# An announced jump for TensorE's expert loop, and the third chunk of gate and up over four column tiles

## The chip, the cores and the metric

The kernel runs on one core of a Trainium2 chip. The metric is the device time of one execution in microseconds. TensorE's full clock is 2.4 GHz; the profile shows the granted clock as a share of it.

## The reference

One inference step of two layers over 256 new and 32 continued frames (288 rows of width 1024), all in float32. Each layer is an attention mix and then a feed-forward part. Layer 0 has a dense SwiGLU, layer 1 a mixture of eight SwiGLU experts, two for each row. The change touches the experts alone:

```python
def moe(h, router, wg, wu, wd):
    logits = jnp.einsum('btd,de->bte', h, router).astype(jnp.float32)
    vals, idx = lax.top_k(logits, TOP_K)
    gates = jax.nn.softmax(vals, axis=-1)
    comb = ...
    for e in range(N_EXPERTS):
        out = out + comb[..., e:e + 1] * swiglu(h, wg[e], wu[e], wd[e])

def swiglu(h, wg, wu, wd):   # wg, wu: 1024 x 2816, wd: 2816 x 1024
    return jnp.einsum('btf,fd->btd', jax.nn.silu(h @ wg) * (h @ wu), wd)
```

## The kernel before, in words

**The experts.** Up to 96 rows (SLOTS) that chose an expert are gathered and worked on together. TensorE's array is cut into four column tiles of 32 (GRAN). Three of them (MAIN) each hold 32 of the 96 rows and multiply the main columns of a weight slice; the fourth does the slice's last columns, the tail, for the three groups in turn. Its results lie in partitions 96 to 127 of PSUM, those of the three main tiles in 0 to 95. The function `lanes` (line 2290) issues this for one slice of 128 weight rows: per PSUM bank of 512 columns first the main tiles (line 2297), then the tails that start in that bank (line 2302). The profile shows each float32 matmul as two passes, each with a weight load (LDWEIGHTS) of 32 columns of the rows; the weights of the expert are what streams.

**Chunks and units.** The 2816 columns of gate and up are cut into chunks of 1024, 1024 and 768 (WIDTH). TAIL is a quarter of the chunk, rounded down to whole 128s: 256, 256 and 128; LANE_W, the main part, is 768, 768 and 640. `project` takes one unit of a chunk, two slices; a chunk has four units of gate and four of up, so 16 slices. `down` multiplies by the down weights in slices of 1024 columns, cut 768 + 256, in four units per chunk (KUNIT: 2, 2, 2, 2 slices, and 2, 2, 1, 1 for the third chunk).

**Between gate/up and down.** ScalarE takes Silu of gate (line 1231), VectorE multiplies by up (line 1752) and gives `act_m`. `turn_chunk` (line 2317) transposes it on TensorE in blocks of 128 columns (line 2321), one transpose for 128 rows where the block has tail rows and one for 96 rows where it has none: 6, 6 and 5 transposes. `turned_parts` (line 557) gives the copies that ScalarE (line 1237) and VectorE (line 1758) then make into `am`: the main rows as they are, the tail rows regrouped into slots behind them.

**Order of the work.** TensorE's order in an expert is written out by hand in `expert(j, final)`: gate and up of chunk 0; half of gate of chunk 1; `turn_chunk(0)`; the rest of gate and up of chunk 1; down of chunk 0; half of gate of chunk 2; `turn_chunk(1)`; the rest of gate and up of chunk 2; `turn_rows` (the next expert's rows, line 2260); down(1,0) and down(1,1); `turn_chunk(2)`; down(1,2) and down(1,3); down of chunk 2.

**The loops.** TensorE, ScalarE, VectorE and GpSimd each have a loop of their own over the experts and the last expert outside it: with one round, seven iterations and one more body, hence six jumps back and one loop exit. The loop of TensorE opens in line 2405:

```python
            last = pe.snap(more * NE + (NE - 1))
            with pe.Fori(0, last) as j:
                expert(j, False)
            expert(last, True)
```

**The weights.** SyncE loads them in units of two slices (1 MB, in the third chunk 768 KB) into a ring of 12 places (line 722). It issues a unit when TensorE has used the one 12 places back (`unit_used`), and TensorE waits for a unit in `wait_unit`. An expert has 36 units.

Of the kernel before, what the change touches and what calls it, by code (L numbers as in the profile page):

```python
# [22 lines left out]
ALU = mybir.AluOpType  # L23
ACT = mybir.ActivationFunctionType
# [35 lines left out]
CHUNKS = (DFF + CW - 1) // CW  # L60
WIDTH = [min(CW, DFF - CW * c) for c in range(CHUNKS)]
KUNIT = [[2, 2, 2, 2], [2, 2, 2, 2], [2, 2, 1, 1]]
TAIL = [w // (MAIN + 1) // P * P for w in WIDTH]
LANE_W = [w - t for w, t in zip(WIDTH, TAIL)]
D_TAIL = D // (MAIN + 1)
D_LANE = D - D_TAIL
SPARE = TOK + P
# [151 lines left out]
def build(nc, a, out, consts):  # L219
# [35 lines left out]
    with ExitStack() as ctx:  # L255
# [123 lines left out]
        slot_row = carve("slot_row", 1, dt=U32)  # L379
        row_at = carve("row_at", 4)  # L380
        xr = carve("xr", D)
        sgm = carve("sgm", max(LANE_W))
        act_m = carve("act_m", max(LANE_W))
        am = carve("am", 2, CW // P, SLOTS)
        y_out = carve("y_out", D)
        sel = carve("sel", 3, P, dt=F32R)
# [166 lines left out]
        def wide(b, rows=P):  # L553

            return ps[0:rows, b:b + 2, :].rearrange("p a b -> p (a b)")

        def turned_parts(c, bank):

            n, m = TAIL[c] // P, LANE_W[c] // P
            s0, s1 = 4 * bank, min(4 * bank + 4, m)  # L560
            src = ps[:, 4 + bank, :].rearrange("p (s c) -> p s c", c=P)
            parts = [(am[:, c % 2, s0:s1, :], src[:, 0:s1 - s0, 0:SLOTS])]
            for i in range(n):
                gs = [g for g in range(MAIN) if s0 <= n * g + i < s1]
                if gs:
                    at_ = n * gs[0] + i - s0
                    dst = am[:, c % 2, m + i, GRAN * gs[0]:GRAN * (gs[-1] + 1)].rearrange("p (g c) -> p g c", c=GRAN)
                    parts.append((dst, src[:, at_:at_ + n * (len(gs) - 1) + 1:n, SLOTS:P]))
            return parts
# [337 lines left out]
        def _(act):  # L907
# [314 lines left out]
            def expert(j, final):  # L1222

                A(warm[:, 0:1], warm[:, 0:1], ACT.Silu)

                def silu(c):

                    act.wait_ge(unit_used, j * len(EXPERT) + (unit["gate", c, 3] + 1))
                    if c:
                        act.wait_ge(act_done, j * CHUNKS + c)  # L1230
                    A(sgm[:, 0:LANE_W[c]], wide(0)[:, 0:LANE_W[c]], ACT.Silu).then_inc(silu_done, 1)

                def turned(c):

                    act.wait_ge(aT_full, j * CHUNKS + (c + 1))
                    for dst, src in turned_parts(c, 0):
                        ins = A(dst, src, ACT.Copy)  # L1237
                    ins.then_inc(aT_first, 1)

                def output():  # L1240

                    act.wait_ge(row_moved, j + 1)
                    act.wait_ge(unit_used, j * len(EXPERT) + len(EXPERT))
                    for g in range(MAIN):
                        ins = A(y_out[GRAN * g:GRAN * g + GRAN, D_LANE:D], wide(6)[SLOTS:P, D_TAIL * g:D_TAIL * g + D_TAIL], ACT.Copy)
                    ins.then_inc(y_tail, 1)
                    A(y_out[0:SLOTS, 0:D_LANE], wide(6)[0:SLOTS, 0:D_LANE], ACT.Copy, scale=slot_gate[0:SLOTS, 0:1])
                    act.wait_ge(y_tail, j + 1)
                    A(y_out[0:SLOTS, D_LANE:D], y_out[0:SLOTS, D_LANE:D], ACT.Copy, scale=slot_gate[0:SLOTS, 0:1]).then_inc(y_taken, 1)

                def last_output():

                    act.wait_ge(row_moved, j + 1)
                    act.wait_ge(y_half, 1)
                    A(y_hi[0:SLOTS, 0:512], ps[0:SLOTS, 6, :], ACT.Copy, scale=slot_gate[0:SLOTS, 0:1]).then_inc(y_high, 1)
                    for g in range(MAIN):
                        if D_TAIL * (g + 1) > 512:
                            act.wait_ge(y_half, 2)
                        ins = A(y_out[GRAN * g:GRAN * g + GRAN, D_LANE:D], wide(6)[SLOTS:P, D_TAIL * g:D_TAIL * g + D_TAIL], ACT.Copy)
                    ins.then_inc(y_tail, 1)  # L1260
                    A(y_hi[0:SLOTS, 512:D_LANE], ps[0:SLOTS, 7, 0:D_LANE - 512], ACT.Copy, scale=slot_gate[0:SLOTS, 0:1]).then_inc(y_high, 1)
                    act.wait_ge(y_tail, j + 1)
                    A(y_hi[0:SLOTS, D_LANE:D], y_out[0:SLOTS, D_LANE:D], ACT.Copy, scale=slot_gate[0:SLOTS, 0:1]).then_inc(y_high, 1)

                silu(0)
                turned(0)
                silu(1)
                turned(1)
                silu(2)
                if not final:  # L1270
                    act.wait_ge(xgT_full, j + 2)
                    tokens_first_half(j + 2, 4)
                turned(2)
                if final:
                    last_output()
                else:
                    output()
# [8 lines left out]
        def _(dve):  # L1286
# [460 lines left out]
            def expert(j, final):  # L1747

                def activations(c):
                    dve.wait_ge(silu_done, j * CHUNKS + (c + 1))  # L1750
                    dve.wait_ge(unit_used, j * len(EXPERT) + (unit["up", c, 3] + 1))
                    V.tensor_tensor(act_m[:, 0:LANE_W[c]], sgm[:, 0:LANE_W[c]], wide(2)[:, 0:LANE_W[c]], ALU.mult).then_inc(act_done, 1)  # L1752

                def turned(c):

                    dve.wait_ge(aT_full, j * CHUNKS + (c + 1))
                    for dst, src in turned_parts(c, 1):
                        ins = V.tensor_copy(dst, src)
                    ins.then_inc(aT_second, 1)

                if not final:
                    picks(bass.ds(j + 1, 1))
                activations(0)
                if not final:
                    dve.wait_ge(row_moved, j + 1)
                    table(j + 2)
                turned(0)
                activations(1)
                turned(1)
                activations(2)  # L1770
                if not final:
                    dve.wait_ge(xgT_full, j + 2)
                    tokens_second_half(5)
                turned(2)
# [29 lines left out]
        def _(pe):  # L1804
# [481 lines left out]
            def expert(j, final):  # L2286
# [2 lines left out]

                    pe.wait_ge(unit_in[u % MOE_RING], j * MOE_FILLS + 16 * (u // MOE_RING + 1))  # L2290

                def lanes(b, x, w, main, tail, first, last):

                    for c0 in range(0, main, 512):
                        c1 = min(c0 + 512, main)
                        for g in range(MAIN):
                            ins = mm_(ps[GRAN * g:GRAN * g + GRAN, b + c0 // 512, 0:c1 - c0], x[:, GRAN * g:GRAN * g + GRAN], w[:, c0:c1],  # L2297
                                      start=first, stop=last)
                        for g in range(MAIN):
                            at_ = tail * g  # L2300
                            if c0 <= at_ < c1:
                                ins = mm_(ps[SLOTS:P, b + c0 // 512, at_ - c0:at_ - c0 + tail], x[:, GRAN * g:GRAN * g + GRAN],  # L2302
                                          w[:, main:main + tail], start=(first and at_ == c0),
                                          stop=(last and (g == MAIN - 1 or at_ + tail >= c1)))
                    return ins

                def project(kind, c, h):

                    u, wd = unit[kind, c, h], WIDTH[c]
                    wait_unit(u)  # L2310
                    w = unit_at(u)[:, 0:2 * wd].rearrange("p (k c) -> p k c", k=2)
                    for k in (2 * h, 2 * h + 1):
                        ins = lanes(0 if kind == "gate" else 2, xg[:, k, :], w[:, k % 2, :], LANE_W[c], TAIL[c], k == 0, k == KD - 1)
                    ins.then_inc(unit_used, 1)

                def turn_chunk(c):

                    pe.wait_ge(act_done, j * CHUNKS + (c + 1))
                    for k in range(LANE_W[c] // P):
                        r = P if k < MAIN * TAIL[c] // P else SLOTS  # L2320
                        ins = tr(ps[:, 4 + k // 4, (k % 4) * P:(k % 4) * P + r], act_m[0:r, k * P:(k + 1) * P], ident[0:r, 0:r])  # L2321
                    ins.then_inc(aT_full, 1)

                def wait_turned(c):
# [4 lines left out]
                def down(c, h):  # L2329
# [3 lines left out]
                    wait_unit(u)  # L2333
                    w = unit_at(u)[:, 0:n * D].rearrange("p (k c) -> p k c", k=n)
                    for k in range(n):
                        ins = lanes(6, am[:, c % 2, k0 + k, :], w[:, k, :], D_LANE, D_TAIL, c == 0 and h == 0 and k == 0, u == len(EXPERT) - 1 and k == n - 1)
                    ins.then_inc(unit_used, 1)

                for half in range(2):
# [62 lines left out]
                    ins.then_inc(y_half, 1)  # L2402

            last = pe.snap(more * NE + (NE - 1))
            with pe.Fori(0, last) as j:
                expert(j, False)
            expert(last, True)

# [78 lines left out]
```

## Time and profile before

| | |
|---|---|
| median of 3 runs | 1301.41 us (1300.61 to 1302.55) |
| the profiled execution | 1301.46 us |
| its span, first to last instruction | 1299.6 us |
| mean granted clock | 0.984 |
| TensorE busy | 1252.6 us, 96% of the span |
| VectorE, ScalarE, GpSimd busy | 24%, 23%, 6% |
| chain that ended last | TensorE 91%, "issue" 3%, VectorE 3%, DMA 2%, ScalarE 2% |
| stretch of the eight experts | from 516.89 us to about 1291 us |

"Issue" is time in which an engine waited for nothing that the profile shows. The chain is followed back from the last instruction. In rows of instructions, PE is TensorE's matmuls, PEld its weight loads, DVE is VectorE, ACT is ScalarE, POOL is GpSimd and SP is SyncE; a q behind the name is that engine's instruction queue. 128*32 is the part of the array in use (rows by columns) and 128x512 the operand that streams through it.

### The profile page before, as it was taken

How to read it: one execution, taken by the hardware profiler on the slowest of the kernel's cores; microseconds unless marked ns; L12 is line 12 of the kernel's file. 1: busy time of each engine (PE TensorE's matmuls, PEld its weight loads, DVE VectorE, ACT ScalarE, POOL GpSimd, SP SyncE). 2: the span in 40 equal slices, each digit the busy share in tenths (PEclk: the TensorE clock that was granted, in tenths of full speed). 3: DMA queues.
4: the chain of work that ended last, by engine and by line, in shares of the span. 5: the costliest groups of instructions: out<-in, count | busy, mean ns of one | idle time of the engine just before them, and what ended most of it. 6: DMA issues, size and time to landing. Idle time of an engine off the chain costs nothing.

```text
span 1299.6 us, 30531 instructions
## 1 busy us (share of the span) xinstructions
PE 1252.6 (96%) x13609; PEld 890.9 (69%) x13609; DVE 314.2 (24%) x632; ACT 301.7 (23%) x594; POOL 78.9 (6%) x175
## 2 busy tenths in 40 slices
PE   8999999999999999998998998998998999899998
PEld 5466799999964756675675675675675675576775
DVE  1677444443335675000000000000000000000001
ACT  2467433332334654001001001001001001000101
POOL 4231000000001020000000000000000000000100
PEclk9999999999999999999999999999999999899999
DMA  8251475544230626999999999999999999999991
GB/s 284 62 145 34 153 236 162 162 146 147 72 119 1 131 100 262 399 405 401 362 346 384 346 354 383 339 358 379 341 353 379 358 344 375 352 350 370 393 404 70
DMA packets 124228, 349.76 MB, mean 269 GB/s; under 512 B 8400, under 2 KB 33840, under 8 KB 124096
## 3 DMA queue, kind: packets, MB, share of 16 engines
q1 hardware_dynamic: 118896, 335.55, 71.8%
q0 software_dynamic: 3648, 10.60, 2.9%
q8 instruction: 118, 1.93, 0.6%
q10 hardware_dynamic: 1552, 1.56, 0.4%
q14 instruction: 14, 0.11, 0.0%
HBM read 339.65 MB, written 8.04 MB: 268 GB/s over the span
## 4 chain that ended last, share of the span: by engine, by line
PE 91%; issue 3%; DVE 3%; DMA 2%; ACT 2%; SPq 0%; DVEq 0%; ACTq 0%
PE ps L2297 34%; PE ps L2302 21%; PE ps L2209 11%; PE ps L1953 8%; PE ps L2225 5%; DMA ring<-in_w_in 2%; PE ps L2321 1%; PE ps L2026 1%; PE ps L2034 1%; PE ps L2086 1%; PE ps L2101 1%; PE ps L2139 1%; PE ps L2149 1%; PE ps L1966 1%; PE ps L2050 1%
## 5 line engine op out<-in xcount | busy, mean ns | idle before, releaser
L2297 PE MATMUL ps<-ring,xg 128*32 128x512 f32 (+2 forms) x2688 | 293.3, 487 | 30.3 <-issue 30.3
L2302 PE MATMUL ps<-ring,xg 128*32 128x256 f32 (+1 forms) x1344 | 277.2, 362 | 0.0
L2297 PE MATMUL ps<-ring_more,xg 128*32 128x512 f32 (+2 forms) x1920 | 200.6, 465 | 0.0
L2297 PEld LDWEIGHTS ps<-ring,xg 128*32 128x32 f32 x2688 | 115.6, 113 | 96.5 <-issue 62.7
L2302 PE MATMUL ps<-ring_more,xg 128*32 128x256 f32 (+1 forms) x960 | 181.7, 338 | 0.0
L2302 PEld LDWEIGHTS ps<-ring,xg 128*32 128x32 f32 x1344 | 145.7, 113 | 34.7 <-issue 5.7
L1752 DVE TENSOR_TENSOR act_m<-sgm,ps 128x768 f32<-128x768 f32 (+1 forms) x24 | 21.8, 909 | 515.4 <-PE ps L2302 415.2
L2302 PE MATMUL ps<-ring_more,am 128*32 128x256 f32 x636 | 140.1, 379 | 0.0
L2297 PE MATMUL ps<-ring_more,am 128*32 128x512 f32 (+1 forms) x1272 | 139.8, 486 | 0.0
L1953 PE MATMUL ps<-ring,hT 128*128 128x512 f32 x256 | 115.2, 596 | 0.3 <-issue 0.2
L2302 PEld LDWEIGHTS ps<-ring_more,xg 128*32 128x32 f32 x960 | 99.5, 110 | 20.3
L2297 PEld LDWEIGHTS ps<-ring_more,xg 128*32 128x32 f32 x1920 | 77.5, 110 | 43.2 <-issue 21.2
L1237 ACT ACTIVATE am<-ps 128x384 f32<-128x384 f32 (+1 forms) x64 | 16.6, 327 | 380.6 <-PE ps L2321 380.6
L2209 PE MATMUL ps<-hT_hi,w_hi 128*128 128x288 f32 x352 | 104.3, 296 | 0.5 <-DVE hT_lo L1645 0.5
L2209 PE MATMUL ps<-hT_lo,w_hi 128*128 128x288 f32 x352 | 103.8, 295 | 0.0
L2209 PE MATMUL ps<-hT_hi,w_lo 128*128 128x288 f32 x352 | 103.5, 294 | 0.0
L1303 DVE TENSOR_TENSOR w_lo<-ring,w_hi 128x2048 fp32r<-128x2048 f32 (+1 forms) x34 | 75.8, 2230 | 96.1 <-ACT w_hi L918 96.1
L2302 PE MATMUL ps<-ring,am 128*32 128x256 f32 x384 | 85.7, 380 | 0.0
L2297 PE MATMUL ps<-ring,am 128*32 128x512 f32 (+1 forms) x768 | 85.6, 486 | 0.0
L2302 PEld LDWEIGHTS ps<-ring_more,am 128*32 128x32 f32 x636 | 69.3, 110 | 22.4
L918 ACT ACTIVATE w_hi<-ring 128x2048 fp32r<-128x2048 f32 (+1 forms) x34 | 63.3, 1863 | 82.2 <-PE ps L2209 44.1
L1953 PEld LDWEIGHTS ps<-ring,hT 128*128 128x128 f32 x256 | 46.9, 190 | 51.9 <-issue 51.7
(358 smaller groups left out, 1558.0 us busy)
## 6 DMA issues: line engine op xcount, KB each, us to landing
ring<-in_moe_w_up SPq DMA_DIRECT2D x48, 1024.0 KB, 7.3
ring_more<-in_moe_w_down SPq DMA_DIRECT2D x48, 1024.0 KB, 8.2
ring<-in_moe_w_gate SPq DMA_DIRECT2D x32, 1024.0 KB, 8.0
ring_more<-in_moe_w_gate SPq DMA_DIRECT2D x32, 1024.0 KB, 8.7
ring<-in_moe_w_down SPq DMA_DIRECT2D x32, 1024.0 KB, 6.9
ring_more<-in_moe_w_gate SPq DMA_DIRECT2D x32, 768.0 KB, 7.4
ring<-in_moe_w_up SPq DMA_DIRECT2D x32, 768.0 KB, 4.9
ring_more<-in_moe_w_up SPq DMA_DIRECT2D x16, 1024.0 KB, 7.6
```

What stands on the lines that cost most here:

```text
L918: A(hi[:, 0:size], src[:, 0:size], ACT.Copy).then_inc(hi_ready, 1)
L1237: ins = A(dst, src, ACT.Copy)
L1303: V.tensor_tensor(lo[:, 0:size], src[:, 0:size], hi[:, 0:size].bitcast(F32), ALU.subtract).then_inc(lo_ready, 1)
L1752: V.tensor_tensor(act_m[:, 0:LANE_W[c]], sgm[:, 0:LANE_W[c]], wide(2)[:, 0:LANE_W[c]], ALU.mult).then_inc(act_done, 1)
L1953: ins = mm_(pair(key), hT[:, k, TOFF[t]:TOFF[t] + P], slot(wk, 4, 512)[:, k % 4, :], start=(k == 0), stop=(k == KD - 1))
L1966: ins = mm_(pair(key)[:, 0:IN_W - S3], hT[:, k, TOFF[t]:TOFF[t] + P], slot(wk, 8, IN_W - S3)[:, k, :], start=(k == 0), stop=(k == KD - 1))
L2026: ins = mm_(pair(key, r)[:, c0:c0 + w], cqT[:, k, TOFF[t]:TOFF[t] + r], slot(("uq", l), 2, 768)[:, k, c0:c0 + w], start=(k == 0), stop=(k ...
L2034: ins = mm_(pair(key, r)[:, c0:c0 + 512], ckvT[:, KOFF[t]:KOFF[t] + r], w_ukv(l, c0 // 512), start=True, stop=True)
L2209: ins = mm_(pair(key)[:, 512 * f:512 * f + TOK], w[:, k, f * P:(f + 1) * P], x[:, k, :], start=(k == 0 and m == 0), stop=(k == KD - 1 and ...
L2225: ins = mm_(pair(("dn", i, d // 2))[:, 512 * (d % 2):512 * (d % 2) + TOK], w[:, k, d * P:(d + 1) * P], x[:, kk, :], start=(kk == 0 and m = ...
L2297: ins = mm_(ps[GRAN * g:GRAN * g + GRAN, b + c0 // 512, 0:c1 - c0], x[:, GRAN * g:GRAN * g + GRAN], w[:, c0:c1], start=first, stop=last)
L2302: ins = mm_(ps[SLOTS:P, b + c0 // 512, at_ - c0:at_ - c0 + tail], x[:, GRAN * g:GRAN * g + GRAN], w[:, main:main + tail], start=(first and ...
```

## The change

The third chunk is divided so that each column tile has 576 columns: main 576, tail 192. The three tails lie in `act_m` and PSUM at TAIL_AT, [64, 256, 576] for the third chunk and where they were for the others. A group's 192 tail columns don't start at whole blocks of 128, so the tail rows of the third chunk are transposed apart: five transposes of the 96 main rows, then six of the 32 tail rows (two banks, three groups). Silu and the product of the third chunk are 768 wide instead of 640.
```diff
-TAIL = [w // (MAIN + 1) // P * P for w in WIDTH]
+HALF = P // 2
+TAIL = [w // (MAIN + 1) for w in WIDTH]
 LANE_W = [w - t for w, t in zip(WIDTH, TAIL)]
+TAIL_AT = [[0, 256, 512], [0, 256, 512], [HALF, 256, 512 + HALF]]
+ACT_W = [max(m, at_[-1] + t) for m, at_, t in zip(LANE_W, TAIL_AT, TAIL)]
...
-        sgm = carve("sgm", max(LANE_W))
-        act_m = carve("act_m", max(LANE_W))
+        sgm = carve("sgm", max(ACT_W))
+        act_m = carve("act_m", max(ACT_W))
...
         def turned_parts(c, bank):
-            n, m = TAIL[c] // P, LANE_W[c] // P
+            m = LANE_W[c] // P
+            src = ps[:, 4 + bank, :].rearrange("p (s c) -> p s c", c=P)
+            if TAIL[c] % P:
+                tails = src[:, 0:MAIN, SLOTS:P]
+                block = am[:, c % 2, m + bank, :].rearrange("p (g c) -> p g c", c=GRAN)
+                if bank == 0:
+                    return [(am[:, c % 2, 0:m, :], src[:, 0:m, 0:SLOTS]), (block[HALF:P], tails[HALF:P])]
+                return [(am[0:HALF, c % 2, m, :], src[0:HALF, 0, 0:SLOTS]), (block, tails)]
+            n = TAIL[c] // P
...
-                    A(sgm[:, 0:LANE_W[c]], wide(0)[:, 0:LANE_W[c]], ACT.Silu).then_inc(silu_done, 1)
+                    A(sgm[:, 0:ACT_W[c]], wide(0)[:, 0:ACT_W[c]], ACT.Silu).then_inc(silu_done, 1)
...
-                    V.tensor_tensor(act_m[:, 0:LANE_W[c]], sgm[:, 0:LANE_W[c]], wide(2)[:, 0:LANE_W[c]], ALU.mult).then_inc(act_done, 1)
+                    V.tensor_tensor(act_m[:, 0:ACT_W[c]], sgm[:, 0:ACT_W[c]], wide(2)[:, 0:ACT_W[c]], ALU.mult).then_inc(act_done, 1)
...
-                def lanes(b, x, w, main, tail, first, last):
+                def lanes(b, x, w, main, tail, tail_at, first, last):
...
-                        for g in range(MAIN):
-                            at_ = tail * g
-                            if c0 <= at_ < c1:
-                                ins = mm_(ps[SLOTS:P, b + c0 // 512, at_ - c0:at_ - c0 + tail], x[:, GRAN * g:GRAN * g + GRAN],
-                                          w[:, main:main + tail], start=(first and at_ == c0),
-                                          stop=(last and (g == MAIN - 1 or at_ + tail >= c1)))
+                        here = [g for g in range(MAIN) if c0 <= tail_at[g] < c0 + 512]
+                        for g in here:
+                            at_ = tail_at[g] - c0
+                            ins = mm_(ps[SLOTS:P, b + c0 // 512, at_:at_ + tail], x[:, GRAN * g:GRAN * g + GRAN], w[:, main:main + tail],
+                                      start=(first and g == here[0]), stop=(last and g == here[-1]))
...
                 def turn_chunk(c):
 
                     pe.wait_ge(act_done, j * CHUNKS + (c + 1))
-                    for k in range(LANE_W[c] // P):
-                        r = P if k < MAIN * TAIL[c] // P else SLOTS
+                    halved = TAIL[c] % P
+                    for k in range((LANE_W[c] + P - 1) // P):
+                        r = SLOTS if halved else P
                         ins = tr(ps[:, 4 + k // 4, (k % 4) * P:(k % 4) * P + r], act_m[0:r, k * P:(k + 1) * P], ident[0:r, 0:r])
+                    if halved:
+                        for bank in range(2):
+                            for g in range(MAIN):
+                                c0 = TAIL_AT[c][g] + (HALF if bank else -HALF)
+                                ins = tr(ps[:, 4 + bank, P * g + SLOTS:P * g + P], act_m[SLOTS:P, c0:c0 + P], ident[SLOTS:P, SLOTS:P])
                     ins.then_inc(aT_full, 1)
...
-            with pe.Fori(0, last) as j:
+            with nc.Fori(0, last, engines=[pe.engine], hint_back_edge=True) as j:
                 expert(j, False)
             expert(last, True)
```

## Rows read from the trace of the kernel before

**Rows 1.** TensorE's waits: engine, line, waited for; us in total, times, longest.

```profile
PE ps L2297 <- issue: 30.3, 7, 5.6
```

**Rows 2.** Timeline (start, us): TensorE at loop entry, first jump, loop exit.

```profile
516.89 0.63 PE L2297 MATMUL ps<-ring,xg 128*32 128x512 f32 x3 [0.26 <-issue]
...
608.11 0.38 PE L2302 MATMUL ps<-ring_more,am 128*32 128x256 f32 x1
613.17 0.63 PE L2297 MATMUL ps<-ring,xg 128*32 128x512 f32 x3 [4.68 <-issue]
...
1201.22 0.39 PE L2297 MATMUL ps<-ring_more,am 128*32 128x256 f32 x3
...
1201.44 0.60 PE L2297 MATMUL ps<-ring,xg 128*32 128x512 f32 x3
```

**Rows 3.** Loop branches: ns min/median/max, first and last start.

```profile
L2405 PEldq COMPARE_BRANCH  x7: 83/6087/7030, 606.9 to 1200.0; - x7
...
L1280 ACTq COMPARE_BRANCH  x7: 40/45/54, 609.8 to 1203.0; - x7
```

**Rows 4.** Stretches: us, TensorE busy (passes), clock, DMA, GB/s; six half-clock ones' sum.

```profile
516.89:608.33 91.44, 91.44 (x1291) 1.00 1.03 404
...
1112.15:1296.00 183.85, 182.24 (x2557) 1.00 0.86 323
589.37:594.55 5.18, 5.18 (x73) 1.00 1.03 409
...
sum 37.55, PE 26.71; mean PE 4.45
```

**Rows 5.** Timeline: a slice of the third chunk and the next's start.

```profile
576.61 0.60 PE L2297 MATMUL ps<-ring_more,xg 128*32 128x512 f32 x3
576.65 0.60 PE L2302 MATMUL ps<-ring_more,xg 128*32 128x128 f32 x4
577.04 0.71 PE L2297 MATMUL ps<-ring_more,xg 128*32 128x512 f32 x6
577.49 0.30 PE L2302 MATMUL ps<-ring_more,xg 128*32 128x128 f32 x1
...
577.69 0.60 PE L2297 MATMUL ps<-ring_more,xg 128*32 128x512 f32 x3
```

**Rows 6.** Timeline: 64-column passes on one column tile, on the whole array.

```profile
480.78 1.09 PE L1830 MATMUL ps<-wr,hT 128*32 128x64 f32 x16
...
504.20 1.00 PE L1830 MATMUL ps<-wr,xT 128*128 128x64 f32 x8
```

**Rows 7.** Timeline and lines: transposes; passes of 128 and 32 rows in turn.

```profile
594.69 0.71 PE L2321 MATMUL ps<-cst,act_m 128*128 128x128 f32 x5
...
588.56 0.88 PE L2260 MATMUL ps<-cst,xr 96*128 96x96 f32 x8
...
469.37 0.68 PE L1865 MATMUL ps<-cst,xres 32*128 32x32 f32 x8
...
L2260 PE MATMUL ps<-cst,xr 96*128 96x96 f32 x56 | 6.2, 253 | 0.0
...
L1865 PE MATMUL ps<-cst,xres 32*128 32x32 f32 x8 | 0.7, 224 | 0.0
...
62.35 0.43 PE L2149 MATMUL ps<-cache_v,pT 128*128 128x64 f32 x2
62.72 0.43 PE L2149 MATMUL ps<-z,pT 32*128 32x64 f32 x2
```

**Rows 8.** Loads: two stretches, as rows 4; DMA view of 516 to 608.

```profile
613.17:711.57 98.40, 93.68 (x1292) 0.97 1.00 363
...
1201.44:1272.00 70.56, 70.56 (x1019) 1.00 1.00 387
...
ring<-in_moe_w_up SPq DMA_DIRECT2D x6, 1024.0 KB, 14.7
...
q8 instruction: 10, 0.16, 0.7%
```

More of the change, by code:

```diff
@@ L557, in turned_parts @@
         def turned_parts(c, bank):
-            n, m = TAIL[c] // P, LANE_W[c] // P
+            m = LANE_W[c] // P
[7 more added lines that the diff above has]
+            n = TAIL[c] // P
             s0, s1 = 4 * bank, min(4 * bank + 4, m)
-            src = ps[:, 4 + bank, :].rearrange("p (s c) -> p s c", c=P)
             parts = [(am[:, c % 2, s0:s1, :], src[:, 0:s1 - s0, 0:SLOTS])]
@@ L2312, in project @@
                     for k in (2 * h, 2 * h + 1):
-                        ins = lanes(0 if kind == "gate" else 2, xg[:, k, :], w[:, k % 2, :], LANE_W[c], TAIL[c], k == 0, k == KD - 1)
+                        ins = lanes(0 if kind == "gate" else 2, xg[:, k, :], w[:, k % 2, :], LANE_W[c], TAIL[c], TAIL_AT[c],
+                                    k == 0, k == KD - 1)
                     ins.then_inc(unit_used, 1)
@@ L2335, in down @@
                     for k in range(n):
-                        ins = lanes(6, am[:, c % 2, k0 + k, :], w[:, k, :], D_LANE, D_TAIL, c == 0 and h == 0 and k == 0, u == len(EXPERT) - 1 and k == n - 1)
+                        ins = lanes(6, am[:, c % 2, k0 + k, :], w[:, k, :], D_LANE, D_TAIL, [D_TAIL * g for g in range(MAIN)],
+                                    c == 0 and h == 0 and k == 0, u == len(EXPERT) - 1 and k == n - 1)
                     ins.then_inc(unit_used, 1)
```

## The prediction

> **What bounds it now.** The shares of busy time come first: TensorE works nearly all of the span and the other engines a quarter of it or less, so a microsecond counts only if it is taken out of TensorE's own stream. The table of waits says where that stream stands still: line 2297 waits seven times for "issue", that is for nothing the profile sees, 30.3 us in all, 5.6 the longest; no DMA of the expert weights is in the list [rows 1]. The timeline puts six of the seven at the back edge of TensorE's expert loop: the last narrow pass of an expert starts at 608.11, the next expert at 613.17. The seventh is the 0.26 us at the loop's entry (516.89). The seventh expert's end, at 1201.44, has no gap: there the loop is left and no jump is taken [rows 2]. The instructions of line 2405 name the cause: seven compare-and-branches, the shortest 83 ns (not taken), the median 6087 ns; ScalarE's branches of its own, short loop take 45 ns [rows 3]. TensorE's body, 1291 matmul passes [rows 4] with as many weight loads, has to fetch its first instructions again at every taken jump. The table of stretches shows what follows: the granted clock falls to 0.50 (1.2 of 2.4 GHz) around each such stop, 37.55 us in six stretches, in which TensorE works for 26.71 us [rows 4].
>
> **Part 1, the announced jump.** It removes the stop at six taken back edges. The idle time is 30.3 - 0.26 = 30.0 us [rows 1, 2]. "Idle" counts from a modelled end 0.38 us after the last pass's start, while passes of this width follow each other 0.22 us apart (1201.22 to 1201.44 in [rows 2]); so the six edges hold 6 x 0.16 = 1.0 us more, 31.0 us. Added are one hint and one jump an iteration. A jump that finds its target should cost what ScalarE's does, 0.05 us and some register work; the branch starts at 606.9 [rows 3], 1.2 us ahead of the last pass, so that is hidden: 0, with 0.5 us an edge (3.0 us) as the other end. **The clock** then has no stop to fall around, as it has none from 1112.15 to 1296.00, across the edge that isn't taken [rows 4]. Work at half speed loses half its time: 26.71 / 2 = 13.4 us. Check: 516.89 to 608.33 is one expert at full clock, 91.44 us [rows 4]; seven are 640.1 us. From 516.89 to 1201.44 [rows 2] it is 684.55 us, 44.5 more, against 31.0 + 13.4 = 44.4.
>
> **Part 2, the third chunk.** A slice (one k of gate or up) now gives three column tiles 512 + 128 columns each and the fourth 3 x 128. Each matmul is two passes. The slice starts at 576.61, its second 512-column pass at 577.04, the next slice at 577.69 [rows 5]: 1.077 us a slice (timeline, a slice further on the same). After the change the main tiles have 512 + 64 and the fourth 3 x 192. Passes of 64 columns on one 32-column tile: sixteen in 1.09 us, the last record itself some 0.22, so (1.09 - 0.22) / 15 = 0.058 us each [rows 6]. Main tile: 2 x 0.43 + 2 x 0.058 = 0.976. Fourth tile: 256 columns take 0.216 us ([rows 2], 0.22), so 192 take 0.163, and six 0.975. The two are even; with a little for uneven ends I take 0.98. There are 16 slices in each of 8 experts: 128 x (1.077 - 0.98) = 12.4 us. Ends: 0 (narrow passes that wait for their weights, below) and 12.9.
>
> Does the fourth tile run free of the others? Its row at 576.65 has four passes while the main tiles are in their first, and it starts one at 577.49, 0.2 us ahead of the next slice's main passes at 577.69. With six fourth-tile passes a slice and eight run in the chunk's first slice, that pass is the next slice's own [rows 5]. The Trainium skill (TensorE: Matmul & The Clock Gate, "The mechanism") states that matmuls start and end strictly in program order; the trace speaks against it here, and by it the saving would be 7.3 us, the rival priced below.
>
> **The turning.** Before: five transposes in 0.71 us, the last record 0.25: (0.71 - 0.25) / 4 = 0.115 each. Eight of 96 rows: (0.88 - 0.25) / 7 = 0.090. Eight of 32 rows: (0.68 - 0.22) / 7 = 0.065 [rows 7]. Old 5 x 0.115 = 0.57, new 5 x 0.090 + 6 x 0.065 = 0.84: +0.27. Between its 96-row and its 32-row part the array changes shape. Where two passes of 128 rows and two of 32 alternate, a pair takes 0.37 us (62.35 to 62.72 [rows 7]); two passes of the kind without a change take 2 x 0.112 (504.20, eight to the last in 1.00 - 0.22 us [rows 6]): 0.14 a change. Sum +0.41 us an expert, all of it on TensorE's path between down(1,1) and down(1,2): 3.3 us in eight. Ends: 2.2 (no price for the change of shape) and 5.5 (0.112 for each of the six). A gain is excluded: eleven are more than five.
>
> **Edits at nothing.** Silu and product of the third chunk are 768 wide instead of 640. TensorE needs the product only after down(1,0) and down(1,1), 5.18 us from 589.37 to 594.55 [rows 4], and the turned rows only after down(1,2) and down(1,3), as long again. That covers some 0.1 us of width on either engine and one more small copy; without the cover it would be about 0.3 us an expert, 2.4 in all. The other matmuls keep order and size; start and stop flags issue nothing.
>
> **Sum.** 31.0 + 13.4 + 12.4 - 3.3 = 53.5 us. The profiled execution took 1301.46 us (span 1299.6), as the median of the runs, 1301.41: 1301.46 - 53.5 = **1248.0 us**.
>
> **What is late next.** An expert then takes 91.44 - 1.55 + 0.41 = 90.3 us and moves what it moves now, 98.40 us x 363 GB/s = 35.7 MB [rows 8]: 396 GB/s. The expert at full clock drew 404 [rows 4]. That leaves 2%. Two units take TensorE 5.18 us [rows 4], so the ring of 12 is 31 us of work, 2.6 of it in use, and a unit lands 14.7 us after its issue at that pace [rows 8]: some 13 us of shortfall are covered.
>
> **Rivals.**
> - *The hint does nothing*, not taken up, or the target lost again from the instruction memory before the jump. For it: no hint is in this trace, and 1291 passes lie between hint and jump. Only part 2 is left: 1301.46 - 12.4 + 3.3 = 1292.4. Chance 0.09.
> - *Half a stop*: the target is there, the block behind it isn't, say 1.5 us an edge with the clock kept: 1257. Against it: after 613.17 no second stop shows, so the first block's work covers a fetch. 0.06.
> - *Narrow passes wait for their weights.* If each cost the 0.112 us that 64 columns cost on the whole array [rows 6], the main tile would need 0.86 + 2 x 0.11 = 1.08, nothing saved: 1260.4. Against it: the 0.058 of [rows 6], where loads are hidden. The Trainium skill (same page and section) lets a load overlap running matmuls only on other rows of the array, which would bring this about. 0.05.
> - *Order over the tiles.* The next slice could start only with the fourth tile's last pass: 0.86 + 0.16 = 1.02, 128 x 0.057 = 7.3 us saved, 1253.1. Against it: [rows 5]. 0.04.
> - *Loads become the bound.* At the 387 GB/s of 1201.44 to 1272.00 [rows 8] an expert would need 92.2 us, 1.9 more; over eight 15 us, less 13 us of cover: 1250, or 1255 if the stops cost clock. 0.04.
> - *Slower.* If holding the announced block took the place of the block fetched ahead, each border between blocks would stop TensorE as the jump does. One expert fetches ten blocks of instructions (516 to 608: 10 packets, 0.16 MB [rows 8]), now without a stop. It decides from 53.5 / 70 = 0.76 us a border over seven iterations; at the 4.68 us of [rows 2] it would be 1576. 0.02.
>
> The forecast has 0.70. **Range:** 1244 (turning and jump at their cheap ends, narrow passes at 12.9, the rest what the rows miss) to 1262, which takes in half a stop, no gain from narrow passes, order over the tiles and late loads. The dead hint and the slower case, 0.11, are left out, and tails. **Signs:** under 0.2%, 2.6 us, can't be told from no change. Faster 0.97 (even the dead hint gives 0.7%), same 0.01, slower 0.02.
>
> **What would show it.** Right: no idle before line 2297 at the six edges and compare-and-branch below 1.2 us; granted clock 1.00 from 517 to the last expert's end; slices of the third chunk 0.98 us apart; the step from down(1,1) to down(1,2) longer by 0.41 us. Wrong: branches near 6 us; slices near 1.02 or 1.08; TensorE idle until a DMA of the ring.

## The result, and the profile after

The changed kernel takes **1262.0 us** (median of 4 runs, 1260.88 to 1263.26) against 1301.75 us for the kernel before in the same comparison: a ratio of 0.9696, 95% interval 0.9679 to 0.9712. The profiled execution took 1260.88 us, its span 1259.0. The forecast was 1248.0 us with a range of 1244 to 1262, and the median, 1262.01, lies just beyond its upper end. The sign and most of the size were right; 14 us of the forecast 53.5 didn't come.

The table of waits (us in total, times, longest), the branches of the loop (ns min/median/max, first and last start) and the timeline around the first jump, of the changed kernel:

```profile
PE ps L2307 <- issue: 7.4, 8, 2.8
```

```profile
L2422 PEldq BRANCH_PREFETCH_HINT  x7: 31/31/55, 516.7 to 1063.9; - x7
L2422 PEldq COMPARE_BRANCH  x7: 88/357/406, 605.9 to 1155.1; - x7
```

```profile
517.05 0.63 PE L2307 MATMUL ps<-ring,xg 128*32 128x512 f32 x3 [0.38 <-issue]
...
607.17 0.38 PE L2312 MATMUL ps<-ring_more,am 128*32 128x256 f32 x1
607.31 0.61 PE L2307 MATMUL ps<-ring,xg 128*32 128x512 f32 x3
...
610.75 0.59 PE L2307 MATMUL ps<-ring,xg 128*32 128x256 f32 x2
612.04 0.41 PE L2307 MATMUL ps<-ring,xg 128*32 128x256 f32 x2 [0.69 <-issue]
612.05 0.40 PE L2312 MATMUL ps<-ring,xg 128*32 128x256 f32 x1
```

The hint does what it says. The branch that took 6087 ns [rows 3] takes 357 ns, and the next expert follows the last one at 607.31 with no gap, where 4.68 us of idle time stood [rows 2]. But the wait for "issue" hasn't gone: 7.4 us in eight pieces are left of 30.3 in seven [rows 1]. One is the loop's entry (0.38). Six look like the one at 612.04: TensorE stops **4.0 us behind the next expert's first pass** (607.31) and goes on at 4.7 us, inside the first units, with nothing to wait for that the profile shows. The eighth and longest stands behind the loop's exit, the place that had no gap before [rows 2]; the timeline there, and the table of stretches (us, TensorE's busy time and passes, its weight loads, the other engines, clock, DMA share, GB/s) for the time behind it:

```profile
1156.49 0.61 PE L2307 MATMUL ps<-ring,xg 128*32 128x512 f32 x3
...
1157.78 1.02 PE L2307 MATMUL ps<-ring,xg 128*32 128x512 f32 x3
1161.64 0.62 PE L2307 MATMUL ps<-ring,xg 128*32 128x512 f32 x2 [2.83 <-issue]
```

```profile
607.30:611.00 3.70, 3.70 (x53) 2.53 (x45) 0.00 (x0) 3.35 (x6) 0.69 (x2) 1.00 1.02 404
...
1162.60:1166.00 3.40, 3.40 (x32) 1.82 (x28) 0.00 (x0) 0.00 (x0) 0.00 (x0) 0.50 1.05 324
```

Read the price of each from starts. The iterations behind a jump take (1156.49 - 607.31) / 6 = 91.53 us, the first one, which has no jump ahead of it, 607.31 - 517.05 = 90.26 us, just what the prediction asked for (90.3). So a stop costs **1.27 us** though only 0.69 is shown idle (ends are modelled), six of them 7.6 us. No clock is lost to them:

```profile
607.31:1156.49 549.18, 544.99 (x7787) 385.96 (x7782) 33.76 (x94) 54.17 (x114) 19.55 (x42) 1.00 1.02 390
```

At the exit the three main tiles start no pass from 1158.2 to 1161.6, and the half-clock stretch that follows costs half of its 3.4 us: 3.8 + 1.7 = **5.5 us**. The 3.8 is the delay of the first pass behind the stop, counted from the last expert's first pass and held against the written-out loop below (e8). The whole comes out the same: from 1156.49 to the end of the span it is 102.5 us, in e8 97.0. Together 13.1 us, of the 14 that are missing.

The third chunk and its turning, in the timeline:

```profile
571.86 0.60 PE L2307 MATMUL ps<-ring_more,xg 128*32 128x512 f32 x3
571.88 0.65 PE L2312 MATMUL ps<-ring_more,xg 128*32 128x192 f32 x3
572.29 0.29 PE L2307 MATMUL ps<-ring_more,xg 128*32 128x64 f32 x6
572.37 0.33 PE L2312 MATMUL ps<-ring_more,xg 128*32 128x192 f32 x1
572.40 0.60 PE L2307 MATMUL ps<-ring_more,xg 128*32 128x512 f32 x3
...
573.37 0.60 PE L2307 MATMUL ps<-ring_more,xg 128*32 128x512 f32 x3
...
593.34 0.63 PE L2332 MATMUL ps<-cst,act_m 96*128 96x96 f32 x5
593.90 0.56 PE L2337 MATMUL ps<-cst,act_m 32*128 32x32 f32 x6
594.39 0.63 PE L2307 MATMUL ps<-ring_more,am 128*32 128x512 f32 x3
```

A slice follows the last after 573.37 - 572.40 = 0.97 us, where it was 1.077 [rows 5]. The six narrow passes of the three main tiles fill 572.29 to 572.40: two per tile in 0.11 us, 0.055 each, so they don't wait for their weights. From the first transpose to the next down pass it is 594.39 - 593.34 = 1.05 us. Before, five transposes stood there in 0.64 us (594.69 [rows 7] to 595.33): forecast +0.41, measured +0.41.

### The profile page after: what moved, and what is told of

It is laid out like the page before. It is cut to its first block, busy times and chain, and to the rows that moved or that the text cites. A ratio compares the mean times of both kernels' runs of the same rounds, so it can differ in the third digit from the quotient of the medians.

```text
span 1259.0 us, 30642 instructions
## 1 busy us (share of the span) xinstructions
PE 1235.7 (98%) x13657; PEld 909.0 (72%) x13657; DVE 316.3 (25%) x640; ACT 303.8 (24%) x594; POOL 79.0 (6%) x175
## 4 chain that ended last, share of the span: by engine, by line
PE 92%; DVE 3%; DMA 2%; ACT 2%; issue 1%; SPq 0%; DVEq 0%; ACTq 0%
PE ps L2307 33%; PE ps L2312 22%; PE ps L2219 11%; PE ps L1963 8%; PE ps L2235 5%; DMA ring<-in_w_in 2%; PE ps L2332 1%; PE ps L2036 1%; PE ps L2044 1%; PE ps L2096 1%; PE ps L2111 1%; PE ps L2149 1%; PE ps L2159 1%; PE ps L1976 1%; PE ps L2060 1%
## 5 line engine op out<-in xcount | busy, mean ns | idle before, releaser
L2307 PE MATMUL ps<-ring,xg 128*32 128x512 f32 (+2 forms) x2688 | 279.1, 465 | 7.4 <-issue 7.4
L2307 PE MATMUL ps<-ring_more,xg 128*32 128x512 f32 (+2 forms) x1920 | 196.6, 454 | 0.0
L2312 PE MATMUL ps<-ring_more,xg 128*32 128x256 f32 (+1 forms) x960 | 193.6, 358 | 0.0
L2312 PEld LDWEIGHTS ps<-ring,xg 128*32 128x32 f32 x1344 | 147.5, 110 | 37.0 <-issue 0.2
L2307 PEld LDWEIGHTS ps<-ring,xg 128*32 128x32 f32 x2688 | 118.7, 110 | 48.3 <-issue 14.0
L1762 DVE TENSOR_TENSOR act_m<-sgm,ps 128x768 f32<-128x768 f32 x24 | 22.9, 954 | 473.6 <-PE ps L2312 473.6
L2312 PEld LDWEIGHTS ps<-ring_more,xg 128*32 128x32 f32 x960 | 103.6, 110 | 27.7
L2307 PEld LDWEIGHTS ps<-ring_more,xg 128*32 128x32 f32 x1920 | 80.0, 110 | 25.0 <-issue 2.7
```

The source lines that it names most:

```text
L1762: V.tensor_tensor(act_m[:, 0:ACT_W[c]], sgm[:, 0:ACT_W[c]], wide(2)[:, 0:ACT_W[c]], ALU.mult).then_inc(act_done, 1)
L2312: ins = mm_(ps[SLOTS:P, b + c0 // 512, at_:at_ + tail], x[:, GRAN * g:GRAN * g + GRAN], w[:, main:main + tail], start=(first and g == here ...
```

## The experiments

**What the stop might be.** Theory: TensorE's instructions come in blocks, and the hint fetches one block, the target's. The block behind it is asked for only once TensorE is in the target's block; when the jump lands late in that block, TensorE runs dry. The profile's list of DMA queues, for two stretches, fits: queue 8 carries instructions, 16 KB a packet, in the first expert ten packets, before [rows 8] and after, in one behind a jump of the changed kernel (607.3 to 698.8) eleven; and one falls between 609.5 and 612.1, just ahead of the restart:

```profile
q8 instruction: 11, 0.18, 0.8%
...
q8 instruction: 1, 0.02, 2.6%
```

### The two parts alone, and two places of the loop's head

```diff
 e1: kernel before
-            with pe.Fori(0, last) as j:
+            with nc.Fori(0, last, engines=[pe.engine], hint_back_edge=True) as j:
 e2: changed kernel
-            with nc.Fori(0, last, engines=[pe.engine], hint_back_edge=True) as j:
+            with pe.Fori(0, last) as j:
 e3, e4: changed kernel
-            with nc.Fori(0, last, engines=[pe.engine], hint_back_edge=True) as j:
+            with nc.Fori(0, last, engines=[pe.engine], hint_back_edge=True, head_slot={pe.engine: 0}) as j:    # e4: 200
```

**e1, the hint alone.** 

> The kernel before with the announced jump alone. Theory (the announced jump is short by two stops the forecast left out: 1.27 us in each of the six iterations behind a jump, when TensorE reaches the end of its first block of instructions, 7.6 us, and 5.5 us at the loop's exit): 1301.4 - 44.4 + 7.6 + 5.5 = 1270.1 us. Rival (the jump saved the whole 44.4 us, and the third chunk is what fell short by 13 us): 1257.0 us.

Measured: 1268.71 us, ratio to before 0.9744 (0.9720 to 0.9767), that is 30 to 36 us saved. The rival's 1257 is out. The loss lies in the hint's part, not in the third chunk.

**e2, the third chunk alone.** 

> The kernel before with the third chunk divided evenly, its jump not announced. Theory (12.1 us gained in the slices, 3.2 us paid for turning): 1301.4 - 12.1 + 3.2 = 1292.5 us, and the idle of some 30 us at the six edges as in the kernel before. Rival (third chunk short by 13 us): about 1305 us.

Measured: 1292.55 us, ratio 0.9933 (0.9911 to 0.9955), that is 6 to 12 us saved. As the theory, and the forecast for this part (9.1 us), had it; the rival's 1305 is out. The waits of the two, e1 above:

```profile
PE ps L2297 <- issue: 6.0, 7, 1.4
PE ps L2302 <- issue: 2.4, 1, 2.4
```

```profile
PE ps L2307 <- issue: 28.6, 8, 4.9
```

**e3, the head at slot 0.** 

> The changed kernel with the loop's first instruction at the start of a fetch block, so that TensorE has a whole block (some 256 instructions, 9 us of work) behind each jump instead of about 100 (3.5 us). Theory (the stop 4 us after the jump is the wait for the block behind the announced one): all six stops go, 1262.0 - 6 x 1.27 = 1254.4 us; the stop at the exit changes its place with the code, not its size by much (5.5 us, 0 to 8). Rival (the stop is tied to the jump itself or to the data, not to the border between blocks): it stays at 4 us after the jump, 1262.0 us.

**e4, the head at slot 200.** 

> The changed kernel with the loop's first instruction at slot 200 of 256: about 56 instructions (2.0 us of work) behind the jump before the next block is needed, instead of about 100 (3.5 us). Theory: the next block comes at the same time after the jump, so each of the six stops is longer by the 1.5 us of work that is missing, 1262.0 + 9 = 1271 us with the clock kept, 1281 us if each stop costs 1.7 us of clock as the one at the exit does. Rival (stop not at the border between blocks): 1262.0 us, stop where it was.

Measured: e3 1269.83 us (ratio 0.9758, 0.9737 to 0.9779), e4 1279.28 us (0.9825, 0.9805 to 0.9846). e4 lies in the range that the theory gave, near its end with lost clock, but in part by luck: of its six stops behind the jumps only three were followed by half clock, and of the 18.4 us that its span is longer 14.5 are theirs, 1.9 the loop's entry's and 2.0 the exit's. At the exit TensorE now stood idle for 4.83 us, right behind the last pass of the loop, and it cost 7.5 us instead of 5.5. e3 was meant to gain 7.6 us and lost 7.8. Its branches and first jump, then the stop of e4:

```profile
L2422 PEldq COMPARE_BRANCH  x8: 88/3294/3655, 518.0 to 1166.8; - x8
...
608.77 0.38 PE L2312 MATMUL ps<-ring_more,am 128*32 128x256 f32 x1
611.56 0.63 PE L2307 MATMUL ps<-ring,xg 128*32 128x512 f32 x3 [2.41 <-issue]
```

```profile
609.22 0.60 PE L2307 MATMUL ps<-ring,xg 128*32 128x512 f32 x3
...
610.94 0.60 PE L2307 MATMUL ps<-ring,xg 128*32 128x512 f32 x3
614.08 0.38 PE L2312 MATMUL ps<-ring,xg 128*32 128x256 f32 x1 [2.54 <-issue]
```

e4 shows the stop moved: the last start ahead of it is 1.7 us behind the next expert's first pass instead of 3.4, and it is longer. (The branches are eight, one more than before: with a placed head a branch leads into the loop too.) In e3 the stop behind the jump is gone, as the theory said, but **a new one stands at the jump itself**. What the theory lacked is the other end of the body. From one branch to the next the trace has 2615 instructions (1297 passes, as many weight loads, 21 others), ten blocks and 55, so with the head at slot 0 the branch lies at slot 54, 55 instructions into its block. The announced target is asked for only when that last block is entered, and at 0.036 us an instruction (2 x 1291 in 91.44 us [rows 4] gives 0.035) those are 2 us. The branch then waits 3.2 to 3.7 us more. The sum, 5.2 to 5.7 us, is near what an unannounced jump costs (6.09 us in the median [rows 3]; the first one's record is 6.05): a block comes 5 to 6 us after it is asked for, announced or not.

The packets of queue 8 bear out when the target is asked for. In the changed kernel one falls between 601.5 and 602.5, some 4 us ahead of the branch at 605.9; in e3 there is none from 604 to 608.5, and the next falls between 608.5 and 609.5, when the branch (607.5 to 611.2) already waits. The two windows, the changed kernel's first:

```profile
q8 instruction: 1, 0.02, 6.5%
...
q8 instruction: 1, 0.02, 6.8%
```

The exit goes by the same count, that of the instructions behind the branch in its block: 1 (e4), some 45 (changed kernel), 201 (e3), with 4.83, 2.83 and 0.40 us idle.

### Both distances at once, the exit, and no loop at all

The theory now has two distances. Behind the jump 256 - s instructions lie ahead of the next block, and s + 54 ahead of the branch in its block (for s up to 201). Both want 6 us, less the lead that TensorE's queue has on the matmuls, an estimate of 1.2 us (from the branch's start at 605.9 to the next expert's first pass at 607.31 it is 1.4, and the branch's own 0.36 lies in it). Slot 104 shares evenly.

```diff
 e5, e6: changed kernel
-            with nc.Fori(0, last, engines=[pe.engine], hint_back_edge=True) as j:
+            with nc.Fori(0, last, engines=[pe.engine], hint_back_edge=True, head_slot={pe.engine: 104}) as j:    # e6: 64
 e7: changed kernel, the loop's branch and counter written by hand so that the hint can take a register
-            with nc.Fori(0, last, engines=[pe.engine], hint_back_edge=True) as j:
+            regs = nc.alloc_registers("moe_j", engines=[pe.engine])
+            leave = nc.alloc_registers("moe_leave", engines=[pe.engine])
+            nc.regs_mov(regs, 0)
+            nc.regs_mov(leave, 0)
+            nc.br("moe_loop", engines=[pe.engine])
+            with nc.body("moe_loop", valid_engines=[pe.engine]):
+                at_top = pe.mark_branch_hint_location(hint=leave[pe.engine] if isinstance(leave, dict) else list(leave)[0])
+                j = nc.snap(regs, min_val=0)
                 expert(j, False)
+                nc.regs_alu(regs, regs, 1, op=ALU.add)
+                nc.regs_alu(leave, regs, last - 1, op=ALU.is_ge)
+                pe.br_lt(regs, last, on_true="moe_loop", on_false="moe_done").branch_hint(at_top)
+            nc.switch_bb("moe_done")
 e8: changed kernel
-            with nc.Fori(0, last, engines=[pe.engine], hint_back_edge=True) as j:
+            for j in range(NE - 1):
                 expert(j, False)
```

**e5, slot 104.** 

> The changed kernel with the loop's first instruction at slot 104 of a fetch block of 256. The body has 2615 instructions, ten blocks and 55, so its branch then lies at slot 158: 152 instructions (5.4 us of work at the 0.036 us of one) behind the jump before the next block is needed, and 158 (5.6 us) between the entry of the last block and the branch. Theory (each block comes 6.05 us after it is asked for, it is asked for when the block before it is entered, and the announced target when the branch's own block is entered; TensorE's queue runs some 1 us ahead of the matmuls): neither the stop behind the jump nor a stop at it, six times 0 to 0.3 us; 97 instructions lie behind the branch at the exit, so a stop there of about 1.3 us instead of 5.5. 1262.0 - 7.6 - 4.2 = 1250 us (up to 1252). Rival (only one of the two distances counts, and the other stop is of another kind): 1257 to 1262 us.

Measured: **1249.99 us**, ratio 0.9611 (0.9597 to 0.9624). As forecast. The branches, and the only stop left behind the entry, at the exit, where 97 instructions follow the branch in its block:

```profile
L2422 PEldq COMPARE_BRANCH  x8: 88/442/471, 516.3 to 1148.1; - x8
...
1152.94 0.38 PE L2307 MATMUL ps<-ring,xg 128*32 128x256 f32 x1
1154.57 0.41 PE L2307 MATMUL ps<-ring,xg 128*32 128x256 f32 x3 [1.25 <-issue]
...
517.10:1149.50 632.40, 632.38 (x9079) 455.88 (x9083) 40.06 (x112) 59.51 (x128) 20.98 (x46) 1.00 1.02 396
```

Over seven experts TensorE is idle for 0.02 us, and a period takes 632.40 / 7 = 90.34 us.

**e6, slot 64.** 

> As before with slot 64: 192 instructions behind the jump (6.9 us), 118 between the entry of the last block and the branch (4.2 us), 137 behind the branch at the exit (4.9 us). Theory: no stop behind the jump; the branch waits 1.0 us in each of six edges (3.3 us less 64 x 0.036), compare-and-branch about 1.3 us; none or a small stop at the exit: 1262.0 - 7.6 + 6.0 - 5.0 = 1255 us. Rival (the wait of the branch in the run with slot 0 is that of a target at a block's start): 1249 us.

```profile
L2422 PEldq COMPARE_BRANCH  x8: 88/1092/1295, 516.9 to 1148.6; - x8
```

Measured: 1250.57 us, ratio 0.9616 (0.9599 to 0.9633), where I expected 1255. The rival's total, 1249, is nearer, but its reason is out: it had the branch not wait, and the branch waits nearly as forecast (1.09 us in the median, 1.3 expected). Only the matmuls don't feel it. I had counted the wait of the branch as lost time and left out the queue's lead, 1.2 us, which covers it. So the place need not be exact: between 64 and 104 no difference can be measured. e3's numbers agree: its first branch's 3.66 us less that lead is the 2.41 us of idle time.

**e7, the hint told of the exit.** 

> The changed kernel, its hint with a register that says in the last iteration that the branch won't be taken; nothing is moved but one instruction ahead of the loop. Theory (the exit stops because the announced target was fetched in place of the block that follows): the stop of 3.4 us at 1158 and the half-clock stretch behind it go, 5.5 us, the six stops behind the jumps stay: 1262.0 - 5.5 = 1256.5 us. Rival (the stop at the exit is that of any branch, announced or not, or of the code behind the loop): 1262.0 us.

```profile
PE ps L2307 <- issue: 5.2, 7, 0.9
...
1161.37 0.61 PE L2307 MATMUL ps<-ring,xg 128*32 128x512 f32 x3
1161.45 0.60 PE L2312 MATMUL ps<-ring,xg 128*32 128x256 f32 x2
1161.80 0.39 PE L2307 MATMUL ps<-ring,xg 128*32 128x256 f32 x3
```

Measured: 1258.31 us, ratio 0.9663 (0.9648 to 0.9679); a little above the 1256.5 expected and below the rival's 1262.0. The profile decides: the last expert starts at 1159.65, passes follow each other without the 3.4 us hole that stood 1.3 us into it, and the half-clock stretch behind the hole is gone. From that start to the end of the span it is 97.1 us, as in e8, against 102.5: the whole 5.5 us. What the total lacks is at the loop's entry, which is new code too: the first expert starts at 518.05 instead of 517.05, its first 3.4 us run at half clock, and it takes 91.9 us instead of 90.26. The six stops behind the jumps remain (5.2 us in seven, the longest 0.9). So the hole was the price of the hint: in the last iteration it fetched the target in place of the block that follows.

**e8, the loop written out.** 

> The changed kernel with TensorE's loop written out seven times: no jump, no branch, the same matmuls. It prices everything that the jumps still cost. Theory (7.6 us in six stops behind the jumps and 5.5 us at the exit are all of it): 1262.0 - 13.1 = 1248.9 us. Rival (long straight code is short of instructions as well, or the loads of the weights become the bound once the stops are gone): 1252 us or more, with idle time before line 2307 or at a DMA of the ring.

```profile
607.35 0.60 PE L2307 MATMUL ps<-ring,xg 128*32 128x512 f32 x3
...
1149.07 0.61 PE L2307 MATMUL ps<-ring,xg 128*32 128x512 f32 x3
```

Measured: **1247.99 us**, ratio 0.9588 (0.9574 to 0.9603). Six experts take 541.72 us, 90.29 each. No wait for "issue" stands in the expert part at all, and none for a weight load. This is the time that the prediction gave, because it is the kernel that the prediction described, one whose jumps cost nothing.

### The version with both cures, and the turning

```diff
 e9: e7, and ahead of the br
+            pe.addr_align(256, offset=104, max_nops=0)
 e10: changed kernel, in turn_chunk
-                    if halved:
+                    if False:
```

**e9, slot 104 and the exit told.** 

> Both cures together: the loop's first instruction at slot 104, and the hint told in the last iteration that the loop will be left. Theory (the written-out loop, 1248.0 us, has no stop; slot 104 leaves 1.6 us at the exit and 0.4 us at the entry): the 1.6 us go, 1250.0 - 1.6 = 1248.4 us, no gap at the exit. Rival (what slot 104 still costs against the written-out loop is spread over the edges, by the branch and the hint): 1250 us.

Measured: 1249.90 us, ratio 0.9607 (0.9594 to 0.9620). In the profile the exit's gap is gone and one stop of 0.9 us at the loop's entry is all that is left:

```profile
PE ps L1931 <- DMA ring<-in_w_in: 1.4, 1, 1.4
...
PE ps L2307 <- issue: 0.9, 1, 0.9
```

The exit was to give 1.6 us, and from the last expert's first pass to the end of the span it is 97.1 us against e5's 98.7. The total is that of the rival, though, and nothing can be told from e5, whose interval it shares. The profiled execution entered the expert loop 1.4 us later than e5's (it waited 1.4 us for weights of the first layer in line 1931, which e5 did not), which hides a gain of 1.6 us. The gain at the exit is shown, in the total it isn't.

**e10, without the six tail transposes.** 

> The changed kernel without the six transposes of the 32 tail rows of the third chunk (their part of the turned rows stays what an earlier chunk left there, so the third chunk's tail columns don't count). It prices the turning apart. Theory (0.065 us for each of six, and 0.14 us for the change of the array's shape): the step from down(1,1) to down(1,2) falls from 1.05 to 0.52 us, 8 x 0.53 = 4.2 us in all, 1257.8 us. Rival (0.112 us for each and nothing for the shape): to 0.38 us, 5.4 us in all. Rival (the six run beside the 96-row ones on their part of the array): it stays at 1.05 us.

```profile
593.36 0.63 PE L2332 MATMUL ps<-cst,act_m 96*128 96x96 f32 x5
593.92 0.63 PE L2307 MATMUL ps<-ring_more,am 128*32 128x512 f32 x3
```

Measured: 1256.1 us in one execution (expected 1257.8), and the step is 0.56 us instead of 1.05. The six cost 0.49, nearer to the theory's 0.53 than to 0.67, the step of the rival. But the five of 96 rows take 0.56 / 5 = 0.112 us each, not 0.090, and the old five, by the same measure, 0.64 / 5 = 0.128, not 0.115. The forecast had the new five 0.11 us too low, the six with their change of shape 0.04 too high, and the old five, which are taken off, 0.07 too low: the three cancel.

## Why the prediction was right and wrong

**The failed step** is the line on the announced jump: "A jump that finds its target should cost what ScalarE's does ... so that is hidden: 0, with 0.5 us an edge (3.0 us) as the other end." The jump itself did that (357 ns, no gap). But the price of a jump isn't only in its target. It was 1.27 us an edge, 7.6 in all, in a stop 4 us into the next expert, and outside both ends given.

The prediction had this as a rival, "half a stop: the target is there, the block behind it isn't", 1.5 us an edge, 1257 us, at 0.06. It was set aside because "after 613.17 no second stop shows, so the first block's work covers a fetch". That reading was the mistake. The stretch behind 613.17 in the kernel before:

```profile
613.17:617.00 3.83, 3.83 (x32) 2.00 (x36) 0.00 (x0) 0.00 (x0) 0.00 (x0) 0.58 1.06 372
613.17:618.30 5.13, 5.13 (x46) 2.60 (x48) 0.00 (x0) 0.00 (x0) 0.00 (x0) 0.67 1.03 332
```

The some 48 passes that the changed kernel starts in 3.7 us (the 53 of its row less the last expert's) took 5.1 there and more, because the stop had halved the clock. The slow work just covered the fetch. Cure the stop, and with it the clock, and the cover is gone. The evidence came from a state that the change was to remove.

**The exit** was in no case. The prediction read "the seventh expert's end, at 1201.44, has no gap" as a place that the change leaves alone. But a hint that says "taken" seven times is wrong once: 5.5 us (e7). The range took in half a stop (1257) but not the exit on top of it, and the two together end at its edge.

**The sum.** Jump idle and clock: 44.4 forecast, less 7.6 and 5.5: 31.3, and e1 measured 30 to 36. That 44.4 was itself right is shown by e8, where jumps are absent, against e2, the same work with unannounced jumps: 1292.55 - 1247.99 = 44.6 us (in two comparisons, in which the kernel before took 1302.6 and 1301.05). e8 lies 53.1 us below the kernel before (1301.05), against the 53.5 of the whole sum; that it meets 1248.0 to the tenth is partly luck.

**Third chunk.** Forecast 12.4 us from slices of 0.98; the slices are 0.97 apart, and the first expert, with no jump ahead, went from 91.44 [rows 4] to 90.26 us although its turning grew by 0.41: 1.59 us gained, 12.7 in eight. Two rivals fell with it. *Order over the tiles* asked for 1.02 a slice. The fourth tile runs free of the others: `lanes` issues two of its passes behind a slice's 64-column ones, but only one (572.37) starts ahead of the next slice's main passes (572.40), the other beside them (572.53). *Narrow passes wait for their weights* asked for 1.08: they take 0.055 us. The Trainium skill (TensorE: Matmul & The Clock Gate, "The mechanism") states both program order and that a load overlaps only matmuls on other rows of the array; for passes on 32-column tiles these rows speak against either. **Turning:** +0.41 forecast and measured, 3.3 us; that the sum came out to the hundredth is luck, since inside it three terms were off and cancelled (e10).

**The other rivals.** *Dead hint*: out, branches at 357 ns. *Loads become the bound*: out; with the experts at 90.3 us the queues move 396 GB/s and TensorE is idle for 0.02 us in 632.40 (e5's stretch). *Every border stops*: out; in e5 some 70 borders pass in 632.40 us with 0.02 us idle.

The number 1248.0 was the time of the likeliest case at 0.70. It was too sure of it: the true case, half a stop, had 0.06, and with the exit that nobody priced it ends at 1262.

## What to carry to other kernels

An announced jump needs room on both sides: work for the time of one fetch between the entry of its last block and the branch, and as much between the loop's head and the end of the target's block. A loop's place in its block can be chosen, and here it was worth 12 us of 1262; the exit wants a hint of its own, or enough work in its block. When a profile is to show that something is covered, ask whether the cover runs at the speed it will have after the change.

## What the runs showed of the hardware

- **A block of instructions comes 5 to 6 us after TensorE asks for it**, and no run shows it asked for more than one block ahead. The unannounced jump waits 6.09 us in the median, 7.03 at most [rows 3]; the branch 55 instructions into its block 3.2 to 3.7 (e3), 119 into it 1.09 (e6), 159 into it 0.44 (e5), against 0.36 where nothing is waited for. The stop behind the jump: about 56 instructions, 2.54 us idle (e4); 100, 0.69; 152, none (e5). The stop at the exit, by the instructions behind the branch in its block: 1, 4.83 us idle (e4); about 45, 2.83 (changed kernel); 97, 1.25 (e5); 137, 0.50 (e6); 201, 0.40 (e3).
- The Trainium skill (Runtime: NRT & Kernel Launch, "Instruction fetch mechanics") has the next block fetched while the present one runs, in blocks of 16 KiB, and a taken branch beyond it as a stall. The packets of 16 KB and the runs agree. It also gives TensorE's instruction memory room for eight such blocks; no run here shows that the room is used to ask for more than the next one. Its advice to write loops out is worth 2.0 us here beyond slot 104.
- **A stop doesn't always cost clock.** In e4 six stops are much alike (13.6 us idle in all, the longest 2.5), and the clock was halved behind three of them. Behind the first, the longest (2.54 us), the clock stays, behind the second (2.21 us) it is halved, as the stretches of e4 show; what sets the two apart no run tells; behind the 0.69 us stops of the changed kernel it never fell.

```profile
PE ps L2312 <- issue: 13.6, 6, 2.5
...
614.10:617.50 3.40, 3.40 (x49) 2.20 (x52) 0.00 (x0) 0.00 (x0) 0.00 (x0) 1.00 1.05 384
708.40:711.80 3.40, 3.40 (x31) 1.89 (x27) 0.00 (x0) 0.00 (x0) 0.00 (x0) 0.50 1.06 351
```

- The queue's lead, an estimate of 1.2 us, hides a wait of that size at a branch (e6).
